# Dealing gathered rows in a zigzag, unmasked expert ranks, first gathers straight from the index table, and separate semaphores for the first returned rows

## The reference

```python
def _moe(h, w_rg, b_rg, w_re, b_re, w_eg, w_eu, w_ed):
    p_group = softmax(hf @ w_rg + b_rg)
    g_star = argmax(p_group)                      # 1 of 4 groups
    top_v, top_i = top_k(e_sel, 2)                # 2 of its 8 experts
    w_top = softmax(top_v) * p_sel
    ...
    # for each expert e of 32:
    #   out += (silu(h @ w_eg[e]) * (h @ w_eu[e]) * combine[:, e]) @ w_ed[e]
...
x = x + _moe(_rmsnorm(x, norm_ffn), ...)
y = _rmsnorm(x, norm_final)
```

## Time and profile before

| | |
|---|---|
| median of 3 runs | 806.15 us (805.64 to 808.15) |
| the profiled execution | 805.87 us, its span 804.0 us, so 1.87 us lie around the span |
| mean granted clock of TensorE | 0.967 |
| PE busy | 723.4 us, 90% |
| DVE busy | 340.9 us, 42% |
| ACT busy | 244.1 us, 30% |
| POOL busy | 82.9 us, 10% |
| moved by DMA | 173.02 MB, 215 GB/s on average |

### The profile page before, as it was taken

One profiled execution on the slowest core, in us unless ns is written; L12 is line 12 of the kernel. 1 busy time (PEld: TensorE's weight loads), 2 busy tenths in 40 slices (PEclk: granted clock), 3 DMA queues, 4 the chain that ended last, 5 costly groups with the idle time before them and its releaser, 6 DMA issues.

```text
span 804.0 us, 12356 instructions
## 1 busy us (share of the span) xinstructions
PE 723.4 (90%) x5112; PEld 538.4 (67%) x5112; DVE 340.9 (42%) x623; ACT 244.1 (30%) x489; POOL 82.9 (10%) x138
## 2 busy tenths in 40 slices
PE   5999999999999999999999999999988787878830
PEld 4888997678999998879999978864433232233310
DVE  6643358655546347343455523732223111111128
ACT  6234374643545333333122241311110010010013
POOL 3404000000000201000000011211112111111200
PEclk9999999999999999999999999999999899999975
DMA  8732111114221713432232299679999999999935
GB/s 315 225 106 62 54 53 53 54 53 136 63 65 53 280 63 144 171 89 83 74 85 93 91 355 386 239 261 398 416 419 418 419 415 404 415 411 419 401 146 220
DMA packets 82631, 173.02 MB, mean 215 GB/s; under 512 B 8064, under 2 KB 42208, under 8 KB 82560
## 3 DMA queue, kind: packets, MB, share of 16 engines
q1 hardware_dynamic: 72736, 148.52, 49.7%
q0 software_dynamic: 9840, 23.72, 7.9%
HBM read 163.26 MB, written 18.74 MB: 226 GB/s over the span
## 4 chain that ended last, share of the span: by engine, by line
PE 66%; DMA 11%; SPq 10%; DVE 8%; ACT 2%; issue 2%; POOLq 0%; ACTq 0%; DVEq 0%
PE bank L737 44%; DMA expert_down<-in_w_exp_down 9%; SPq L544 7%; PE bank L1189 5%; PE bank L1205 4%; SPq L549 2%; DVE w_split L1548 2%; ACT w_split L1243 1%; PE bank L757 1%; PE bank L1128 1%; PE bank L1114 1%; PE bank L1022 1%; PE bank L1028 1%; DVE s_state L1846 1%; DMA token_out<-token_out_scratch 1%
## 5 line engine op out<-in xcount | busy, mean ns | idle before, releaser
L737 PE MATMUL bank<-hT_split,w_split 128*128 128x272 f32 x1152 | 154.1, 292 | 0.0
L737 PEld LDWEIGHTS bank<-hT_split,w_split 128*128 128x128 f32 x1152 | 147.3, 188 | 2.1 <-issue 0.9
L737 PE MATMUL bank<-w_split,hT_split 128*128 128x512 f32 (+1 forms) x576 | 130.1, 380 | 0.5 <-DVE w_split L1548 0.5
L1189 PE MATMUL bank<-expert_gate_up,gatheredT 128*64 128x512 f32 x512 | 113.3, 593 | 3.7 <-DMA expert_gate_up<-in_w_exp_up 2.8
L737 PEld LDWEIGHTS bank<-w_split,hT_split 128*128 128x128 f32 x576 | 100.1, 188 | 22.9 <-issue 3.3
L1548 DVE TENSOR_TENSOR w_split<-w_raw,w_split 128x2048 fp32r<-128x2048 f32 (+1 forms) x35 | 75.9, 2168 | 83.1 <-ACT w_split L1243 83.1
L1205 PE MATMUL bank<-expert_down,expert_actT 128*64 128x512 f32 x256 | 69.6, 694 | 30.9 <-DMA expert_down<-in_w_exp_down 27.5
L1189 PEld LDWEIGHTS bank<-expert_gate_up,gatheredT 128*64 128x64 f32 x512 | 38.8, 137 | 75.0 <-issue 69.5
L1243 ACT ACTIVATE w_split<-w_raw 128x2048 fp32r<-128x2048 f32 (+1 forms) x35 | 63.4, 1812 | 42.4 <-PE bank L737 17.5
L1205 PEld LDWEIGHTS bank<-expert_down,expert_actT 128*64 128x64 f32 x256 | 20.9, 156 | 68.6 <-issue 38.7
L737 PE MATMUL bank<-gla_outT_split,w_split 128*128 128x272 f32 x384 | 49.4, 288 | 0.0
(11 more groups left out here) (355 smaller groups left out, 838.6 us busy)
## 6 DMA issues: line engine op xcount, KB each, us to landing
expert_gate_up<-in_w_exp_gate SPq DMA_DIRECT2D x64, 512.0 KB, 14.7
expert_gate_up<-in_w_exp_up SPq DMA_DIRECT2D x64, 512.0 KB, 15.7
expert_down<-in_w_exp_down SPq DMA_DIRECT2D x32, 1024.0 KB, 17.0
w_raw<-in_w_in SPq DMA_DIRECT2D x15, 1024.0 KB, 5.5
w_raw<-in_w_in SPq DMA_DIRECT2D x16, 512.0 KB, 4.7
s_state<-in_state_gla POOLq DMA_DIRECT2D x4, 1024.0 KB, 8.7
out_sample_gla_state<-s_state POOLq DMA_DIRECT2D x4, 1024.0 KB, 6.3
w_raw<-in_w_proj_gla SPq DMA_DIRECT2D x8, 512.0 KB, 4.2
```

The source lines that it names most:

```text
L737: ins = mm(out, stat(x, k), mov(y, k), start=first and n == 0 and m == 0, stop=last and n == len(ks) - 1 and m == 2)
L1189: ins = mm(P[2 + u][64 * half:64 * half + 64, :].rearrange("p (m n) -> p m n", m=2), XT[u][:, k, 64 * half:64 * half + 64], WGU[gb][:, k / ...
```

## The change

Four things are changed.

1. `slot_row` is another permutation. Slot p of a half lies in group p // 8 and has lap p % 8; it holds rank 8 lap + group on even laps and 8 lap + 7 - group on odd ones. Ranks are dealt over the eight groups of eight neighbouring slots, to and fro.
2. Ranks of odd experts begin at `ODD` = 1024 and no longer at 64, and `slot_row` of the upper 64 slots begins there too. A rank over 63 then matches no slot, so the comparison and the addition (L1975, L1976) are gone, and `chosen` reads the ranks from PSUM.
3. The first two gathers take their indices from a column of `IDXG` itself; the two copies on POOL ahead of them are gone. `columns` is counted up by POOL itself so that later waits keep their numbers.
4. At the end y1 of blocks 0 and 1 counts on a semaphore of its own, and DVE waits for it ahead of L2107 and for y2 only ahead of L2109.

Fillers: 5 instead of 7 after the ranks, 9 instead of 12 after the slot table. The changed kernel leaves out no part of the computation.

```diff
-SPREAD, UNSPREAD = 39, 23
+ODD = 1024
...
-    parts["half_row"] = np.broadcast_to(CAP * (e % 2), (128, NE))
-    parts["half_end"] = np.broadcast_to(CAP + CAP * (e % 2), (128, NE))
+    parts["half_row"] = np.broadcast_to(ODD * (e % 2), (128, NE))
...
-    parts["slot_row"] = np.broadcast_to(CAP * (p // CAP) + UNSPREAD * p % CAP, (128, 128))
+    group, lap = p % CAP // 8, p % 8
+    parts["slot_row"] = np.broadcast_to(ODD * (p // CAP) + 8 * lap + np.where(lap % 2, 7 - group, group), (128, 128))
...
+                    landed = first_in[bl] if k == 0 and bl < 2 else x_in[bl]
                     sp.dma_start(YI[2 * bl + k][0:rows(bl), :],
-                                 tok_d[k * NTOK + bl * 128:k * NTOK + bl * 128 + rows(bl), :]).then_inc(x_in[bl], 16)
+                                 tok_d[k * NTOK + bl * 128:k * NTOK + bl * 128 + rows(bl), :]).then_inc(landed, 16)
...
             for u in range(2):
-                pool.tensor_copy(ICG[u][:], IDXG[:, u:u + 1]).then_inc(columns, 1)
-            for u in range(2):
-                pool.wait_ge(columns, 3 + u)
-                gather(u, ICG[u])
+                pool.sem_inc(columns, 1)
+                gather(u, IDXG[:, u:u + 1])
...
-            keep_clock(7)
+            keep_clock(5)
...
-            keep_clock(12)
+            keep_clock(9)
...
-            link(V.tensor_tensor(tmp, ranks, per_expert(cst("half_end")), ALU.is_ge))
-            link(V.scalar_tensor_tensor(out=sent, in0=tmp, scalar=1000.0, in1=ranks, op0=ALU.mult, op1=ALU.add))
-            chosen(R2["fixed"], sent, PROD)
+            chosen(R2["fixed"], ranks, PROD)
...
-                dve.wait_ge(x_in[bl], 16 + 32)
+                if bl < 2:
+                    dve.wait_ge(first_in[bl], 16)
+                else:
+                    dve.wait_ge(x_in[bl], 16 + 32)
                 link(V.scalar_tensor_tensor(out=y1[0:n, :], in0=y1[0:n, :], scalar=R1["w1"][0:n, bl:bl + 1], in1=X2[0:n, bl, :],
                                             op0=ALU.mult, op1=ALU.add))
+                if bl < 2:
+                    dve.wait_ge(x_in[bl], 16 + 16)
```

More of the change, by code:

```diff
@@ L71, in shape_constants @@
     parts["pairsteps"] = np.broadcast_to(2 * np.arange(OVH // 2), (128, OVH // 2))
-    assert (SPREAD * UNSPREAD) % CAP == 1
-    parts["slot_row"] = np.broadcast_to(CAP * (p // CAP) + UNSPREAD * p % CAP, (128, 128))
+    group, lap = p % CAP // 8, p % 8
+    parts["slot_row"] = np.broadcast_to(ODD * (p // CAP) + 8 * lap + np.where(lap % 2, 7 - group, group), (128, 128))
     parts["over_pair"] = np.broadcast_to(np.arange(NFIX, NFIX + OVH), (128, OVH))
@@ L192, in decoder_step @@
     T0 = W0 + 20480
-    RR = [at(f"route_{n}", [128, NB, NE], F, T0 + 640 * n) for n in range(3)]
+    RR = [at(f"route_{n}", [128, NB, NE], F, T0 + 640 * n) for n in range(2)]
     PROD = at("route_products", [128, 2, NB, NE], F, T0 + 1920)
@@ L468, in decoder_step @@
         out_stored = sem("out_stored")
+        first_in = [sem("first_in0"), sem("first_in1")]
         STEP, count = {}, 0
@@ L678, in gather @@
                 pool.indirect_dma_start(out=XG[u][:], out_offset=None, in_=h2_d,
-                                        in_offset=bass.IndirectOffsetOnAxis(ap=col[:], axis=0),
+                                        in_offset=bass.IndirectOffsetOnAxis(ap=col, axis=0),
                                         bounds_check=NTOK - 1, oob_is_err=False).then_inc(gathered[u], 16)
             for u in range(2):
-                pool.tensor_copy(ICG[u][:], IDXG[:, u:u + 1]).then_inc(columns, 1)
-            for u in range(2):
-                pool.wait_ge(columns, 3 + u)
-                gather(u, ICG[u])
+                pool.sem_inc(columns, 1)
+                gather(u, IDXG[:, u:u + 1])
             pool.wait_ge(rows_ready, 2)
@@ L699, in move_rows @@
                 pool.sem_inc(pool_passed, 1)
-                gather(u, ICG[u])
+                gather(u, ICG[u][:])
                 pool.wait_ge(y_out_a, n + 2)
@@ L1943, in _ @@
             lg, le = LG[:, :, 0:NG], LG[:, :, NG:36]
-            ge, tmp, sent = RR[0][:], RR[1][:], RR[2][:]
+            ge, tmp = RR[0][:], RR[1][:]
             mark_first_of_max(lg, RG[0][:], R1["gmax"], R1["grev"], cst("rev4"), NG)
@@ L2031, in over_places @@
                 link(V.tensor_scalar(R2["half"][:], R2["tile"][:], float(OVH), None, ALU.is_ge))
-                link(V.scalar_tensor_tensor(out=R2["row"][:], in0=R2["half"][:], scalar=float(CAP), in1=R2["row"][:], op0=ALU.mult, op1=ALU.add))
+                link(V.scalar_tensor_tensor(out=R2["row"][:], in0=R2["half"][:], scalar=float(ODD), in1=R2["row"][:], op0=ALU.mult, op1=ALU.add))
                 link(V.scalar_tensor_tensor(out=R2["a"][:], in0=R2["half"][:], scalar=-float(OVH), in1=R2["tile"][:], op0=ALU.mult, op1=ALU.add))
```

## The result

The changed kernel takes 822.49 us (median of 4 runs, 820.96 to 825.48) against 805.89 us before in the same comparison: a ratio of 1.0204, 95% interval 1.0167 to 1.0242. It is 16.6 us slower. The forecast was 801.6, so it failed in sign. The profiled execution took 820.96 us, its span 819.1.

A forecast was written before the change was run, and what follows sets the result against it. The DMA engines were taken to bound the expert stage. Gains of 1.2 ahead of it, 2.1 from dealing and 1.2 from returned rows, 4.5 us off 805.87, gave 801.4, forecast as a median of 801.6, range 800.2 to 803.0.

The forecast's parts named there:

- Part 1: Routing chain on DVE: without the two masked instructions, L1970 starts and the chain shifts 0.71 us sooner.
- the bound of 0.1: Routing chain: reading ranks from PSUM costs L1970 between 0 and 0.1 us more; 0 was taken.
- Part 2: Before the first gather: without the two POOL copies 0.34 to 0.48 us go; 0.34 was taken.
- The head: Routing up to the first gather: masked instructions 0.71 plus POOL copies 0.34, together 1.05 us sooner.
- What starts sooner: Ahead of the expert stage: 1.05 us plus 0.15 for one row less on the second gather's fullest engine, 1.2 us.
- Part 3: Expert stage: ranks dealt over eight neighbouring slots per engine relieve the fullest engine; 2.1 us gained, bounds 0 and 4.2.
- the trace's support: End of the expert stage: about two engines working alone for 2.4 us were taken to speak for eight neighbours.
- the missing share of 4.6 us: Run-dry tail of the expert stage: the DMA share missing there, 4.6 us, is the most perfect balance could give.
- The first rival: Expert stage: four neighbouring slots and four 32 above share an engine; 12.7 us more there, kernel 816.6; chance 0.08.
- The clock rival: First pair: fewer fillers and idle PE lower the clock, slowing matmuls that release SP; 1.7 us, 803.3; chance 0.03.
- Part 4: Returned rows at the end: DVE starts with the first landed load, 1.2 us gained, bounds 0.9 to 1.3.
- Rows don't set the late engines: Rival, expert stage: the dealing gives nothing and 2.25 us of gains remain, 803.9; chance 0.13.

The follow-up runs named there:

- the balanced kernel: Kernel before with only the ranks dealt to and fro over groups of four neighbouring slots and the four 32 above: 806.80 us, ratio 0.9999.
- the quads: Changed kernel with ranks dealt to and fro over groups of four neighbouring slots and the four 32 above: 805.54 us, ratio 0.9975.
- the run with 176: Kernel before with ranks in order, slot_row = p, 176 transfers on the fullest engine: 809.57 us, ratio 1.0034.
- the one with two heavy engines: Kernel before with ranks 0 to 7 always in slots 0 to 3 and 32 to 35, 232 transfers on engines 0 and 8: 822.35 us, ratio 1.0197.

## Why the prediction was wrong

- **Part 1, the masked instructions: right.** 0.71 us forecast; from the selection to the end of the instruction that writes the index table there are 0.70 us less (4.99 for 5.69). The product from PSUM takes 0.48 us against 0.49 from SBUF, so the bound of 0.1 wasn't needed.
- **Part 2, the copies on POOL: mechanism right, term mis-sized.** 0.34 us forecast, 0.2 found: from the end of L1993 (527.54) to the gather (528.56) 1.02 us pass, not 0.88. The head is worth 0.9 us instead of 1.05.
- **"What starts sooner", one row less on the second gather: wrong**, by the same false rule as part 3. The fullest engine had 8 rows in both gathers where it had 6 and 5 before, both landed about 0.7 us later after their issue, and SP's first down weights left at 534.38 and not at 533.35. Of these 1.03 us, 0.3 are a later selection, which the change doesn't touch.
- **Part 3, the dealing: the step that failed.** It says "Here I have to assume ... I take eight neighbouring slots to one engine". The runs show four and four. By that rule the fullest engine went from 141 to 222 transfers and not from 154 to 127, and the term that stood in the sum as 2.1 us gained was, measured alone, 18.5 us lost. What I called the trace's support, 1.6 engines in the last 2.4 us of the earlier trace rows, doesn't tell the rules apart: the balanced kernel has the same 0.10. Nor does the missing share of 4.6 us: by the same sum over its tail (1.00, 0.82, 0.38, 0.10) the balanced kernel misses 3.6. So this sum doesn't say what balance can give; dealt by the right rule it gave 0.1 us.
- **The first rival, weighed at 0.08, is what happened.** Its price was 816.6 us; 822.5 were measured. Its 12.7 us in the stage were 14.3 in the profile, and 1.5 of these stand in the last gate and up matmuls alone, 5.15 us instead of 3.65, at a granted clock of 0.50 after a wait of 2.47. Left out of its sum were also, with the sizes of the table, the longer first gathers (0.4), the longer last scatter (0.4) and the slow first pair (2.0, which the run with 12 fillers did not win back). Of its observable signs two came true: PE waited longer for the first gathered rows (2.07 us) and for down weights (36.4 us for 27.5). In mid-stage PE waited for no gather, and the share hardly fell: it stays at 0.99 to 1.01 in mid-stage, and it is the rate that falls.
- **The clock rival: right in kind, wrong in worth.** The clock did fall in the first pair and delayed SP by 2.0 us, near the 1.7 that the rival gave it, but taking the delay away brought no gain. It came with a wait of 2.07 us where 0.9 was forecast; with the old permutation the wait is 1.07 and the clock stays, so it took the dealing's later gathers as well as the shorter fillers.
- **Part 4, the returned rows: right.** 1.2 us forecast, 1.3 measured alone (0.5 to 2.1). Only the wait between y1 and y2 of block 0, named as a sign, didn't come.
- **"Rows don't set the late engines" (0.13)** is right for small differences: 127 against 141 transfers buys nothing. Had the dealing followed the right rule, the ratio would have been the 0.9975 of the quads, which of this comparison's 805.89 is 803.9: that rival's price and not my 801.6.

## What to carry to other kernels

An assumption on which slots share a DMA engine has to be tested with a permutation that separates the rules before rows are dealt by it; a probe costs one line. Look at the height of the share's plateau where the transfers run out: it counts the engines left (0.50 for eight, 0.13 for two), but a short tail of one or two engines is there in balanced kernels too. Dealing finer than some 15 transfers in 120 wasn't worth anything here, while dealing wrong cost 2%.

## What the runs showed of the hardware that I had not expected

- Of the three rules tried, only one has every run on the right side: an indirect DMA over 128 slots puts slots 4k to 4k + 3 and 4k + 32 to 4k + 35 of each half of 64 on one engine (k from 0 to 7), skipped slots counted in: the dealing over eight neighbours costs 18.5 us, over these groups nothing (ratio 0.9999).
- The price of imbalance against the fullest engine's transfers in the stage, all against 141: 127 and 137: 0 (-0.1 and -0.5 us); 176: +2.7; 198: +9.3, with about 1.5 of slow clock in it; 222: +18.5 with the dealing alone; 232: +15.9 on two engines, +20.5 where more are heavy. At 0.157 us a transfer it would be -2.2, -0.6, +5.5, +9.0, +12.7 and +14.3. Why the run with 176 comes out cheaper than its transfers and those from 222 on dearer is not settled. In the dear ones the engines stay busy at a lower rate: 375 GB/s at a share of 0.99 in the changed kernel, 355 at 0.98 in the one with two heavy engines:

```profile
680.00:720.00 40.00, 28.18 (x116) 10.05 (x116) 5.38 (x13) 3.16 (x6) 4.68 (x8) 0.87 0.98 355
```

Engines that are busy and move less have packets that take longer. That these are the light engines' packets, and that the heavy ones hold them back, is my reading; no run took it apart.
